# Four norms in two parts of the tokens, with 384-token ranges and weight splits taken ahead, in a two-block kernel on Trainium2

## The chip, the cores and the metric

The kernel runs on one core of one Trainium2 chip. The metric is device time in microseconds (us) of one execution. A core has TensorE (PE; its weight loads are shown apart as PEld), VectorE (DVE), ScalarE (ACT), GpSimd (POOL) and SyncE (SP), which here issues nearly all DMAs.

## The reference, cut to what matters

A first block (three mixers, output projection, MLP with squared relu) works on 512 tokens, then a second block of two layers on 512 tokens ("x") and 256 context tokens ("c"). Model width is 1024. Around the change this is computed (l is the layer of the second block):

```python
# first block
x = x + mix @ w_out
h2 = rmsnorm(x, norm2_w)                                  # "n2"
x = x + jnp.square(jax.nn.relu(h2 @ w_ff1)) @ w_ff2
# second block, l = 0 (x and context), then l = 1 (only x after the attention)
hx = modulate(rms_norm(x, norm1_g[l]), sh1, sc1)          # "n3" for l=0, "l1n1" for l=1
px = hx @ w_in[l]                                         # conv inputs, latents, fourier inputs
x = x + g1 * heads_out(att_x, px, hy, w_out[l])
x = x + g2 * sq_relu_mlp(modulate(rms_norm(x, norm2_g[l]), sh2, sc2), w_mlp1[l], w_mlp2[l])  # "l0n2", "l1n2"
```

rms_norm divides each token by the root of the mean of its squares over the 1024 features. In layer 1 the context is only needed up to keys and values, so "l1n1" norms 768 tokens and "l1n2" 512.

## The kernel before, in words

Activations lie feature-major: X is [128 partitions, 8 tiles of features, 768 tokens], the first 512 being x, the last 256 the context. Each weight matrix comes in tiles of 128x1024 fp32 through a ring of 5 (`weight_ring`), loaded by SP in the order of `loads` (`fill`, L2982). Each product is made of three fp32r products: ACT casts a tile to its high part (`split_hi`, L2182, row L2193) and DVE, or for every third tile POOL (`lo_of`), takes the low part (`split_lo`, L1352 and L2733, rows L1362 and L2743), into a ring of 4 (`WS`, "weight_split"). The activations have a high and a low part too. A slot of WS is free when the product four tiles earlier is done. `stage` on each engine splits up to two tiles ahead (AHEAD = 2).

TensorE's order is written out by hand, and each other engine has a program of its own that goes through the same steps; semaphores (`did`, `when`) tie them. `product` (L663, matmuls in L685) makes one 128-feature output tile over k = 0..7 and three parts; the token ranges are XB = (0..512, 512..768) where the context takes part and X1 = (0..512) elsewhere, so a range is one matmul with its own weight load. `product_as_made` (L635, matmuls in L654) makes two output tiles at once while the norm still makes the inputs: step k waits for the high part of feature tile k, and its low part is used a step later.

A norm stands between the output projection and the MLP (n2, l0n2, l1n2), or between the MLP and the next layer's in-projection (l1n1):

- DVE adds each output tile to X (`out_projection`, L1694; in the MLP L1738), ACT squares it (L2206), DVE sums the squares (L1373).
- TensorE's `norm` (L626) sums over partitions (`token_sums`, L603), filler matmuls (`keep_busy`, L589) keep it at work, ACT takes the root (L2211), DVE the reciprocal (L1378), TensorE spreads it to all partitions (L620).
- `normed_split` on DVE (L1380; L1388 scales, L1400 or L1402 takes the low part of even tiles), ACT (L2218; L2224 or L2226 makes the high part, L2230 the shifted whole of odd tiles) and POOL (L2748, L2753: the low part of odd tiles) makes the split inputs of the next product tile by tile, with two buffers in SQ.

All tokens go through a norm together, after the last output tile. `mlp` (TensorE L926) makes groups of 4 hidden tiles ("up", L685) and, one group later, adds them into X ("down", L949); the relu and the square of a hidden tile are made once for each range (ACT L2442 and L2446, POOL L2864, DVE L1721). Layer 0's down products run beside `late_modulation` on DVE (L1450).

SP's program stops at two norms: after w_ff1 tile 2 it waits until n2 has scaled its last tile (`n2_vec ("scaled", 7)`), loads two broadcast rows, and goes on with weights and modulation weights in turn; at l0n2 it waits for the last low parts.

In both attentions the first two tiles of w_out2 are split when head 7 begins (`feed`, L2094 and L2647: `split_hi`, `split_lo` up to `w_out2` 0 + 1). `mid` is the stage before the attention (spectra, values). The end of `attention_2` makes the first two output tiles as the mixes come (`out_pair`, L1292), and `MIX2` is the order of their k.

## Time and profile before

| | us |
|---|---|
| median of 3 timed runs | 2395.6 (2392.7 to 2411.45) |
| the profiled execution | 2409.31 |
| its span | 2407.5 |
| PE busy | 2305.8 (96% of the span) |
| DVE busy | 1409.9 (59%) |
| ACT busy | 901.5 (37%) |
| POOL busy | 514.6 (21%) |
| DMA | mean 95 GB/s, 227.69 MB |

Starts and windows are microseconds from the span's first instruction; durations in groups are ns of one instruction. A matmul's duration is from its issue to its modelled end, so back-to-back matmuls overlap and their pace is read from starts. In brackets stands how long the engine had been idle, and what ended that.

### The profile page before, as it was taken

How to read it: one execution, taken by the hardware profiler on the slowest of the kernel's cores; microseconds unless marked ns; L12 is line 12 of the kernel's file. 1: busy time of each engine (PE TensorE's matmuls, PEld its weight loads, DVE VectorE, ACT ScalarE, POOL GpSimd, SP SyncE). 2: the span in 40 equal slices, each digit the busy share in tenths (PEclk: the TensorE clock that was granted, in tenths of full speed). 3: DMA queues.
4: the chain of work that ended last, by engine and by line, in shares of the span. 5: the costliest groups of instructions: out<-in, count | busy, mean ns of one | idle time of the engine just before them, and what ended most of it. 6: DMA issues, size and time to landing. Idle time of an engine off the chain costs nothing.

```text
span 2407.5 us, 29863 instructions
## 1 busy us (share of the span) xinstructions
PE 2305.8 (96%) x11514; PEld 1828.8 (76%) x11514; DVE 1409.9 (59%) x2253; ACT 901.5 (37%) x1536; POOL 514.6 (21%) x385
## 2 busy tenths in 40 slices
PE   7989799999999998989999999999999999999998
PEld 5655577888877875668888888888776568888887
DVE  5475648888667456773565565543635774534435
ACT  4254533232333224882422222122422684423232
POOL 2332214232312210001312121111120001322221
PEclk9999899999999999999999999999999999999999
DMA  4211016555411221011243343321122112222321
GB/s 162 88 62 54 27 35 235 193 192 203 167 66 57 93 96 34 22 36 36 84 140 123 118 136 123 123 101 59 58 96 80 32 45 70 102 89 96 109 88 53
DMA packets 76248, 227.69 MB, mean 95 GB/s; under 512 B 9151, under 2 KB 12608, under 8 KB 76108
## 3 DMA queue, kind: packets, MB, share of 16 engines
q1 hardware_dynamic: 70928, 216.69, 26.5%
q0 software_dynamic: 1856, 6.07, 0.7%
q10 hardware_dynamic: 3324, 3.02, 0.4%
q8 instruction: 93, 1.52, 0.3%
q14 instruction: 47, 0.39, 0.1%
HBM read 220.99 MB, written 4.76 MB: 94 GB/s over the span
## 4 chain that ended last, share of the span: by engine, by line
PE 84%; DVE 7%; ACT 4%; issue 3%; POOL 2%; ACTq 0%; DMA 0%; DVEq 0%; SPq 0%; POOLq 0%
PE psum L685 33%; PE psum L949 25%; PE psum L1256 3%; PE psum L715 3%; PE psum L654 3%; PE psum L1287 2%; PE psum L735 2%; PE psum L1210 2%; PE psum L1145 1%; PE psum L1271 1%; PE psum L603 1%; PE psum L1104 1%; PE psum L1223 1%; PE psum L1171 1%; DVE mod_scratch L1440 1%
## 5 line engine op out<-in xcount | busy, mean ns | idle before, releaser
L685 PE MATMUL psum<-mix_split,weight_split 128*128 128x512 f32 (+1 forms) x3456 | 701.3, 364 | 2.3 <-POOL weight_split L2743 1.3
L685 PEld LDWEIGHTS psum<-mix_split,weight_split 128*128 128x128 f32 x3456 | 589.8, 188 | 110.4 <-POOL weight_split L2743 1.7
L949 PE MATMUL psum<-hidden,weight_split 128*128 128x512 f32 (+1 forms) x3072 | 623.2, 364 | 0.6 <-DVE residual L1736 0.6
L949 PEld LDWEIGHTS psum<-hidden,weight_split 128*128 128x128 f32 x3072 | 523.5, 188 | 96.9 <-DVE weight_split L1362 1.0
L2193 ACT CAST weight_split<-weight_ring 128x1024 fp32r<-128x1024 f32 x269 | 277.1, 1041 | 298.4 <-PE psum L949 235.6
L2743 POOL TENSOR_TENSOR weight_split<-weight_ring,weight_split 128x1024 fp32r<-128x1024 f32 x89 | 233.0, 2618 | 597.1 <-ACT weight_split L2193 596.5
L1721 DVE TENSOR_TENSOR hidden<-hidden_tmp,hidden 128x512 fp32r<-128x512 f32 (+1 forms) x128 | 156.0, 1238 | 305.9 <-POOL hidden_tmp L2864 305.9
L1362 DVE TENSOR_TENSOR weight_split<-weight_ring,weight_split 128x1024 fp32r<-128x1024 f32 x180 | 233.8, 1301 | 39.8 <-ACT weight_split L2193 39.8
L2864 POOL TENSOR_TENSOR hidden_tmp<-hidden_tmp 128x512 f32<-128x512 f32 (+1 forms) x128 | 127.5, 1007 | 598.3 <-ACT hidden L2446 598.0
L2442 ACT ACTIVATE hidden_tmp<-psum 128x512 f32<-128x512 f32 (+1 forms) x128 | 69.2, 541 | 482.8 <-PE psum L685 481.8
L1738 DVE SCALAR_TENSOR_TENSOR residual<-psum,modulation,residual 128x512 f32<-128x512 f32 x192 | 120.2, 657 | 156.3 <-PE psum L949 155.9
L685 PE MATMUL psum<-normed_in,weight_split 128*128 128x512 f32 (+1 forms) x936 | 186.7, 360 | 6.7 <-POOL weight_split L2743 3.6
L685 PEld LDWEIGHTS psum<-normed_in,weight_split 128*128 128x128 f32 x936 | 154.6, 194 | 41.9 <-DVE weight_split L1362 7.4
L1440 DVE CUSTOM_DVE_ANT_0 mod_scratch<-mod_ring,cond 128x1024 f32<-128x1024 f32 x96 | 130.7, 1362 | 1.7
L1256 PE MATMUL psum<-k_heads,q_heads 128*128 128x512 f32 (+1 forms) x288 | 107.4, 494 | 9.4 <-ACT mla_prob L2665 5.6
L2206 ACT ACTIVATE squares<-residual 128x512 f32<-128x512 f32 (+2 forms) x60 | 39.5, 659 | 180.7 <-DVE residual L1706 72.2
L715 PE MATMUL psum<-normed,weight_split 128*128 128x512 f32 x360 | 96.9, 421 | 6.0 <-ACT q_and_k L2344 4.5
L715 PEld LDWEIGHTS psum<-normed,weight_split 128*128 128x128 f32 x360 | 69.9, 201 | 32.9 <-issue 17.5
L1256 PEld LDWEIGHTS psum<-k_heads,q_heads 128*128 128x128 f32 x288 | 52.2, 195 | 52.7 <-issue 42.3
L2123 DVE TENSOR_TENSOR mla_probT<-psum,mla_probT 128x256 fp32r<-128x256 f32 (+1 forms) x144 | 72.0, 537 | 18.0 <-ACT mla_probT L2679 17.1
L2112 DVE TENSOR_REDUCE mla_stat<-psum 128x1 f32<-128x768 f32 (+1 forms) x80 | 67.7, 846 | 25.0 <-PE psum L1256 23.9
L2446 ACT ACTIVATE hidden<-hidden_tmp 128x512 fp32r<-128x512 f32 (+1 forms) x128 | 74.0, 578 | 8.4
(317 smaller groups left out, 2483.7 us busy)
## 6 DMA issues: line engine op xcount, KB each, us to landing
weight_ring<-in_w_mlp SPq DMA_DIRECT2D x128, 512.0 KB, 3.8
weight_ring<-in_w_ff SPq DMA_DIRECT2D x64, 512.0 KB, 4.4
mod_ring<-in_w_mod SPq DMA_DIRECT2D x48, 512.0 KB, 3.5
late_ring<-in_w_mod SPq DMA_DIRECT2D x96, 256.0 KB, 3.4
weight_ring<-in_w_in SPq DMA_DIRECT2D x45, 512.0 KB, 3.5
weight_ring<-in_w_out SPq DMA_DIRECT2D x24, 512.0 KB, 3.4
weight_ring<-in_tables SPq DMA_DIRECT2D x13, 512.0 KB, 3.5
weight_ring<-in_w_v SPq DMA_DIRECT2D x8, 512.0 KB, 3.9
```

Source lines behind the costliest of these rows:

```text
L685: m = pe.matmul(psum[:, b + r, 0:hi - lo], w[:, part_w, :], x[:, part_x, k, lo:hi], start=k == 0 and part_w + part_x == 0, stop=k == KT - ...
L715: m = pe.matmul(bank(b), w[:, part_w, :], HS_1[:, part_x, k, :], start=k == 0 and part_w + part_x == 0, stop=k == KT - 1 and part_w == 1)
L949: mm = pe.matmul(psum[:, b + r, 0:hi - lo], w[:, part_w, :], G[:, part_x, f % (2 * GROUP), lo:hi], start=jj == 0 and part_w + part_x == 0, ...
L1256: m = pe.matmul(psum[:, b + off // 512, 0:pw], QH[:, h % 3, q:q + P], KH[:, h % 3, k0 + off:k0 + off + pw], start=True, stop=True)
L1362: ve.tensor_tensor(WS[:, k, 1, 0:w], ring_of(i, 0, w), WS[:, k, 0, 0:w].bitcast(F32), ALU.subtract).then_inc(*did("split_lo_vec", j))
L1440: ve.tensor_tensor_reduce(out=mod_scratch[:, :], in0=mod_ring[:, n % 4, :], in1=cond[:, v, :], scale=1.0, scalar=0.0, op0=ALU.mult, op1=AL ...
L1721: ve.tensor_tensor(G[:, 1, k, a:z], act_tmp[:, f % 2, a:z], G[:, 0, k, a:z].bitcast(F32), ALU.subtract).then_inc(*did(tag + "_vec", ("lo", ...
L1738: ve.scalar_tensor_tensor(out=x, in0=ps, scalar=gate(m + i, a), in1=x, op0=ALU.mult, op1=ALU.add).then_inc(*did(tag + "_vec", ("down", g - ...
L2193: ac.copy(WS[:, j % SPLIT_RING, 0, 0:w], ring_of(i, 0, w)).then_inc(*did("split_hi", j))
L2446: ac.activation(G[:, 0, k, a:z], x, ACT.Square).then_inc(*did(tag + "_act", ("hi", f, r)))
L2743: po.tensor_tensor(WS[:, k, 1, 0:w], ring_of(i, 0, w), WS[:, k, 0, 0:w].bitcast(F32), ALU.subtract).then_inc(*did("split_lo_pool", j))
L2864: po.tensor_tensor(x, x, x, ALU.mult).then_inc(*did(tag + "_pool", ("square", f, r)))
```

## The change

It has five parts.

1. **Norms in two parts of the tokens.** n2 and l1n2 are cut into tokens 0..256 and 256..512, l0n2 and l1n1 into 0..512 and 512..768. The last four output tiles (of the last down group, all eight) are made first for part a, then for part b. Part a's sums come after tile (4, b) and its spread after (5, b) ((1, b) and (3, b) in the down group), and its `normed_part` runs beside the rest of part b's tiles. The first pair of the next product is made first over part a, then over part b, with part b's sums and spread between its steps. `keep_busy` is gone from these four norms.
2. **384-token ranges.** In layer 0's output projection (its first four tiles) and MLP (from hidden tile 2 on, down groups 0 to 6) the two ranges are 0..384 and 384..768. Relu, square and low part of a hidden tile are then one instruction over 768 tokens, and a residual add is three (`pieces_of`: 384, 128 and 256 wide).
3. **Splits ahead of the norm.** The first three weight tiles after a norm are split between the steps of its part a and part b (`last + 1` to `last + 3`).
4. **Splits ahead of the attention.** w_out2 tiles 0 and 1 are asked for at the start of `mid`, so that the stage-ahead rule splits them at the end of the in-projection, not in the attention.
5. SP waits for part b of n2 and of l0n2 where it waited for the whole norm.

```diff
-        LAST_APART = {"n1", "n2", "n3", "n3g", "l0n2", "l1n1", "l1n2", "fin"}
+        LAST_APART = {"n1", "n3", "n3g", "fin"}
+        PARTED = 4
+        def parts_of(norm):
+            cut = S if norm in ("l0n2", "l1n1") else S // 2
+            return [(norm + "a", 0, cut), (norm + "b", cut, T2 if cut == S else S)]
+        def up_spans(ranges, f):
+            return XB if len(ranges) > 1 and f < 2 else [(0, ranges[-1][1])]
+        def halves_of(l):
+            return X1 if l else [(0, T2 // 2), (T2 // 2, T2)]
...
+            def out_and_norm(tag, tiles, x, norm, order=range(KT)):
+                for i, p in product_in_parts(tag, tiles, x, [part[1:] for part in parts_of(norm)], order):
+                    if (i, p) == (4, 1):
+                        part_sums(norm, 0)
+                    if (i, p) == (5, 1):
+                        part_spread(norm, 0)
+            def pair_in_parts(tag, tiles, x, norm, evac, sums_at, spread_at):
...
+                for p, (part, lo, hi) in enumerate(parts_of(norm)):
...
+                    for step, _ in enumerate(steps):
+                        if (p, step) == (0, sums_at):
+                            part_sums(norm, 1)
+                        if (p, step) == (0, spread_at):
+                            part_spread(norm, 1)
...
+                                sums_at, spread_at = (1, 4) if len(ranges) > 1 else (2, 6)
...
 # TensorE, mid
+                for m in range(2):
+                    use_load("w_out2", (l, m), split=True)
...
 # VectorE, out_projection
+                add_part(4, 1)
+                inverse_part(norm, 0)
+                split_lo(last + 1)
+                add_part(5, 1)
+                split_lo(last + 2)
+                for t, _ in enumerate(normed_part(norm, 0, HS, gain, shift)):
+                    if t == 1:
+                        add_part(6, 1)
+                    if t == 3:
+                        add_part(7, 1)
+                inverse_part(norm, 1)
+                split_lo(last + 3)
+                for _ in normed_part(norm, 1, HS, gain, shift):
+                    pass
...
 # VectorE and ScalarE, attention
-                    if first and h == MH - 1:
-                        split_lo(load_at["w_out2", (l, 0)] + 1)
...
 # SyncE
-            sy.wait_ge(*when("n2_vec", ("scaled", KT - 1, 0)))
+            sy.wait_ge(*when("n2b_vec", ("scaled", KT - 1, 0)))
```

## Rows read from the trace of the kernel before

**Rows 1.** The page, part 4: shares of the chain that ended last, by engine.
```profile
PE 84%; DVE 7%; ACT 4%; issue 3%; POOL 2%; ACTq 0%; DMA 0%; DVEq 0%; SPq 0%; POOLq 0%
```

**Rows 2.** The chain in order of time, merged: start us, us, what.
```profile
1102.24 50.16 PE psum L685 x288
...
1228.99 33.92 PE psum L949 x192
...
2089.47 21.76 PE psum L949 x96
```

**Rows 3.** Timeline inside the second attention: start us, us, engine, line, tiles, shapes, count.
```profile
1926.06 1.20 PE L1287 MATMUL psum<-mla_probT,weight_split 128*128 128x256 f32 x8
...
1927.09 0.64 PE L1287 MATMUL psum<-mla_probT,v_heads 128*128 128x256 f32 x4
...
1927.56 1.03 PE L1223 MATMUL psum<-latents,weight_ring 128*128 128x256 f32 x4
```

**Rows 4.** Timeline at the norm l0n2 (brackets: idle before, releaser).
```profile
1152.34 1.48 PE L603 MATMUL psum<-squares,c_row 128*6 128x128 f32 x12
...
1156.42 0.94 DVE L1378 RECIPROCAL squares<-squares 6x128 f32<-6x128 f32 x1 [2.84 <-ACT squares L2211]
...
1160.88 17.24 PE L654 MATMUL psum<-mix_split,weight_split 128*128 128x512 f32 x96
...
1177.95 2.28 PE L685 MATMUL psum<-mix_split,weight_split 128*128 128x512 f32 x12
```

**Rows 5.** VectorE groups by form, 1100 to 1240 us: busy us, mean ns of one, idle before.
```profile
L1388 DVE SCALAR_TENSOR_TENSOR squares<-residual,gain_scale,psum 128x512 f32<-128x512 f32 x8 | 5.9, 744 | 1.3 <-PE psum L620 1.3
...
L1388 DVE SCALAR_TENSOR_TENSOR squares<-residual,gain_scale,psum 128x256 f32<-128x256 f32 x8 | 3.8, 476 | 0.0
```

**Rows 6.** Timeline at the norm n2.
```profile
345.40 1.04 PE L603 MATMUL psum<-squares,c_row 128*4 128x128 f32 x8
...
361.57 1.67 SPq L2994 DMA_DIRECT2D weight_ring<-in_w_ff  x3
...
365.11 7.14 PE L685 MATMUL psum<-mix_split,weight_split 128*128 128x512 f32 x30 [1.32 <-POOL weight_split L2743]
...
368.73 1.23 DVE L1362 TENSOR_TENSOR weight_split<-weight_ring,weight_split 128x1024 fp32r<-128x1024 f32 x1 [7.44 <-ACT weight_split L2193]
```

**Rows 7.** Timeline at the norm l1n2.
```profile
2038.44 1.04 PE L603 MATMUL psum<-squares,c_row 128*4 128x128 f32 x8
...
2056.67 3.56 PE L685 MATMUL psum<-mix_split,weight_split 128*128 128x512 f32 x15
```

**Rows 8.** Timeline at the norm l1n1 and the products after it.
```profile
1703.80 1.48 PE L603 MATMUL psum<-squares,c_row 128*6 128x128 f32 x12
...
1728.17 2.11 PE L685 MATMUL psum<-normed_in,weight_split 128*128 128x512 f32 x8 [2.54 <-POOL weight_split L2743]
...
1741.32 1.04 PE L993 MATMUL psum<-filter_h,s_fw 64*64 64x512 f32 x2 [0.74 <-ACT filter_h L2497]
```

**Rows 9.** Timeline inside the two attentions, at the early weight splits.
```profile
1064.68 2.80 PE L1256 MATMUL psum<-k_heads,q_heads 128*128 128x512 f32 x4 [2.59 <-ACT mla_prob L2665]
...
1965.09 1.20 PE L1287 MATMUL psum<-mla_probT,weight_split 128*128 128x256 f32 x8
...
1970.41 1.20 PE L1287 MATMUL psum<-mla_probT,weight_split 128*128 128x256 f32 x8
...
1971.33 2.00 ACT L2193 CAST weight_split<-weight_ring 128x1024 fp32r<-128x1024 f32 x2
...
1977.51 0.69 PE L1271 MATMUL psum<-c_ident,mla_prob 128*128 128x128 f32 x2 [3.70 <-DVE mla_probT L2123]
...
1981.92 1.67 PE L1287 MATMUL psum<-mla_probT,weight_split 128*128 128x256 f32 x8
```

**Rows 10.** Busy in a window: us, PE, PEld, DVE, ACT, POOL, clock, DMA, GB/s.
```profile
1805.00:1825.00 20.00, 20.00 (x97) 16.20 (x97) 7.10 (x9) 4.84 (x7) 0.34 (x1) 1.00 0.08 27
```

**Rows 11.** The page, part 5: the weight loads of L685.
```profile
L685 PEld LDWEIGHTS psum<-mix_split,weight_split 128*128 128x128 f32 x3456 | 589.8, 188 | 110.4 <-POOL weight_split L2743 1.7
```

More of the change, by code:

```diff
@@ L164 @@
 VEC, VECS = vec_plan()
+PART_OF = {f"{norm}{part}_{engine}": (f"{norm}_{engine}", part)
+           for norm in ("n2", "l0n2", "l1n1", "l1n2") for part in "ab" for engine in ("pe", "vec", "act", "pool")}
 class Ledger:
@@ L633, in norm, with product_as_made @@
                 freed[b] = freed[b + 1] = [last]
-            def product_as_made(tag, tiles, x, ranges, x_ready, evac, bs, at, order=range(KT)):
+            def product_as_made(tag, tiles, x, ranges, x_ready, evac, bs, at, order=range(KT), places=None, ends=True):
                 for k in range(KT + 1):
@@ L691, in product, with product_in_parts @@
                                 freed[b + r] = [evac(i, r)]
+            def product_in_parts(tag, tiles, x, spans, order=range(KT)):
+                at = [use_load(*w, split=True) for _, w in tiles]
+                for p, (lo, hi) in enumerate(spans):
+                    for (i, _), load in zip(tiles, at):
+                        j = split_at[load]
+                        b = bank_of[tag, i, p] = take()
+                        if p == 0:
+                            pe.wait_ge(*when(lo_of(j), j))
+                        wait_bank(b)
+                        for k in range(KT):
+                            w = WS[:, j % SPLIT_RING, :, order[k] * P:(order[k] + 1) * P]
+                            for part_w, part_x in ((0, 0), (0, 1), (1, 0)):
+                                m = pe.matmul(psum[:, b, 0:hi - lo], w[:, part_w, :], x[:, part_x, k, lo:hi],
+                                              start=k == 0 and part_w + part_x == 0, stop=k == KT - 1 and part_w == 1)
+                        m.then_inc(*did("gemm", (tag, i, p)))
+                        freed[b] = [(tag + "_vec", ("add", i, ("part", p)))]
+                        split_use[j] = (tag, i, p)
+                        yield i, p
@@ new lines, in out_and_norm @@
+            def out_and_norm(tag, tiles, x, norm, order=range(KT)):
[5 more added lines that the diff above has]
+            def pair_in_parts(tag, tiles, x, norm, evac, sums_at, spread_at):
+                bs = []
+                for i, _ in tiles:
+                    bs.append(take(2))
+                    bank_of[tag, i] = bs[-1]
+                at = [use_load(*w, split=True) for _, w in tiles]
+                for p, (part, lo, hi) in enumerate(parts_of(norm)):
+                    place = (0, 0) if p == 0 else (1, 0) if lo == S else (0, lo)
+                    steps = product_as_made(tag, tiles, x, [(lo, hi)], lambda k: part_ready(part, k), evac, bs, at, places=[place], ends=p == 1)
+                    for step, _ in enumerate(steps):
[3 more added lines that the diff above has]
+                            part_spread(norm, 1)
@@ L1322, in block_2 @@
                 RG = ranges_of(l)
-                if l == 1:
-                    norm("l1n1", 6, ("l1n1_vec", ("scaled", 7, 1)))
                 in_projection_2(l, "n3" if l == 0 else "l1n1")
@@ L1380, in normed_split, with normed_steps @@
             def normed_split(tag, HS, ranges, gain, shift, what="spread"):
+                for _ in normed_steps(tag, HS, ranges, gain, shift, what):
+                    pass
+            def normed_steps(tag, HS, ranges, gain, shift, what="spread"):
                 def scaled(t):
@@ L2423, in out_projection, with mlp @@
                     for m in ms:
-                        ac.wait_ge(*when(tag + "_vec", ("add", m, len(ranges) - 1)))
+                        ac.wait_ge(*when(tag + "_vec", ("add", m, last_piece(ranges, len(ranges) - 1))))
                         square(norm_tag, m, X[:, m, :], [SQ[:, 0, :], SQ[:, 1, :]], 0, ranges[-1][1])
-            def mlp(tag, w1, w2, G, act_tmp, ranges, work, sums, gained=None):
+            def mlp(tag, w1, w2, G, act_tmp, ranges, work, sums, gained=None, next_norm=None):
                 hi = ranges[-1][1]
@@ L2650, in feed @@
                     first = k0 == 0 and i == 0
-                    if first and h == MH - 1:
-                        split_hi(load_at["w_out2", (l, 0)] + 1)
                     if first and h % 2 == 0:
```

426 lines of the change are left out of this document (323 added, 103 removed).

## The prediction

> **What bounds the kernel now.** I read the page first: the chain that ended last lies on TensorE for 84% of the span [rows 1]. What can be won is TensorE's own pace, and the places where it waits or runs filler. The chain in order of time shows the pace [rows 2]. Where only 512 tokens are made, 96 matmuls take 21.76 us, 226.7 ns each. In layer 0's MLP, 96 pairs of a 512- and a 256-token matmul take 33.92 us, 353.3 ns a pair. The same kind of pair in layer 0's output projection is faster: 144 pairs in 50.16 us, 348.3 ns with the start and the end of the stretch in it, about 347 without. 256-token fp32r matmuls alone are seen in the attention: 8 of them from 1926.06 to 1927.09 (129 ns each), 4 from 1927.09 to 1927.56 (118 ns) [rows 3]. So N columns cost about N/2.4 ns + 13.3 (226.7 at 512, 120 at 256), and a 256-token matmul sometimes 7 to 9 ns more.
>
> Then the timeline at the four norms, from the first sums to the third product after the norm, where there should be only two products' work [rows 4, 6 to 8].
>
> **The 384-token ranges.** By that formula 384 columns are 173.3 ns and a pair 346.7, as the faster 512/256 pairs have; it saves 6.7 ns against 353.3. The pairs: up 30 tiles x 24 = 720, down 7 groups x 8 x 12 = 672; 1392 x 6.67 ns = 9.3 us. The output projection's four tiles already run at 346.7 and gain nothing. No row shows an fp32r matmul of 384 columns. From below, the excess of 6.7 ns may not come from the short range and stay: 0. From above I let it save twice as much, if the 13.3 is smaller too: 18. I take 9.3, since the 7 to 9 ns extra is seen on 256-column matmuls and not on 512-column ones.
>
> What a matmul costs apart from its columns can be set against a rule. The Trainium skill ("TensorE: Matmul & The Clock Gate", section Back-to-back issue gap) gives a warm matmul N/2.4 + 2.5 ns, a fixed cost that does not depend on how 768 columns are cut in two. By it the cut to 384 saves nothing; the rows agree neither on the 2.5 (they show 13.3) nor on its being fixed (353.3 beside 346.7 for the same columns). It is the first rival below.
>
> The other engines have room: a residual add becomes three instructions for two on DVE, some 0.2 us per tile of 4.2, and relu, square and low part become one for two; nothing of it is waited for. If that cover were gone, 56 tiles x 0.2 = 11 us would be the price.
>
> **The norms.** I set out each stretch in two clocks and let t = 0 be the end of tile (7, a), when all of part a's residual is made.
>
> *l0n2* [rows 4]. Before: four output tiles 4 x 24 x 0.3467 = 33.3; sums, fillers, root, reciprocal, spread 1152.34 to 1160.88 = 8.5; the pair to 1177.95 = 17.1; together 58.9. After: part a of four tiles 4 x 24 x 0.2267 = 21.8. From t = 0: (4, b) 2.9, sums 0.9, (5, b) 2.9, spread 0.5, (6, b) and (7, b) 5.8, so TensorE is at the pair at 13.0. Meanwhile ACT's root and DVE's reciprocal (0.94) end at 5.2, the add of (5, b) waits for the product (6.7), the split of the second weight tile (cast 1.04, low part 1.23) ends at 9.9, and part a's first tile is ready at 11.4: in time. But part b's sums stand at step 1 of the pair (TensorE at 15.3), and they need the add of (7, b), which on DVE stands behind two splits, the steps 0 to 3 of part a's norm (3 x 0.74 for two tiles [rows 5], 2.4 us with the hops between engines) and the add and sum of (6, b): it comes at 16.9, its square at 17.4. A stall of 2.1. Part b's root on ACT is queued behind all of part a's high parts (21.5), the reciprocal ends at 22.9, TensorE is at the spread at 22.0: a stall of 1.0. Part b runs at 3 x 0.48 us of DVE for two tiles [rows 5], no slower than TensorE's 0.72 a tile. The pair ends at 33.5. 58.9 - 21.8 - 33.5 = 3.6; 0.3 off for the slower 256-column matmuls: 3.3 gained.
>
> *n2* [rows 6]. Before: 21.8 + 19.7 (345.40 to 365.11) = 41.5. After: four tiles of part a at 2.88 = 11.5. The same walk gives the pair's start at 12.35, its part a until 20.2 (two stalls of 0.6), and part b bound by the norm: the chain scale, high part, low part on POOL takes, by an estimate from the 0.48 of DVE and half of what 512 tokens take on ACT and POOL, 1.7 us for two tiles, TensorE 1.44. The end is at 28.0. This is 39.5, but 256-column matmuls at 127 instead of 120 take back 1.0, and then comes SP: it waits for part b's last scaled tile and only then asks for w_ff1 tile 3. Before, that tile was asked for at 361.57 and its low part done at 369.96, 8.4 later, while TensorE needed it at 370.5, since it still had the waiting POOL split and tile 2 to do. Now TensorE ends the pair some 1.5 us behind the last scaled tile and tile 2 5.4 us after; it waits about 2.3 us. Together 42.8: 1 us lost.
>
> *l1n2* [rows 7]. Before 21.8 + 18.2 (2038.44 to 2056.67) = 40.0. After, no SP wait, and ACT's shifted parts pace part b: 11.5 + 27.5 = 39.0. 1 us gained.
>
> *l1n1* [rows 8]. Before: the last down group 33.9, then 1703.80 to 1728.17 = 24.4 (the pair's steps waited for ACT and the third weight tile for POOL's split, 2.54); 58.3. After: 21.8 for part a; from t = 0 sums at 2.9, (2, b) and (3, b) to 6.7, spread, the rest of part b to 13.0. DVE's norm of part a is broken by four adds with their sums, so step 2 waits 1.8 and the sums of part b 1.0; the pair ends at 28.2, and the third tile, split by POOL behind the root, is ready at 28.4. 58.3 - 50.2 = 8.1. Some of it goes back: part b's norm then still lies on DVE and ACT until about 33, ahead of the convolutions of the first two tiles and of the split of the fourth weight tile, needed at 35 and ready at 38.9. Behind it lies the filter chain, for which TensorE waits already (0.74 at 1741.32). I take off 3.9: 4.2 gained.
>
> The norms together: 3.3 - 1.0 + 1.0 + 4.2 = 7.5. Bounds: at worst the rate of the norm rules each pair and nothing is gained (0, and down to -5 with lower clock after each stall, as no filler stands there any more); at best every stall goes: the stretches less the pairs' own work are 8.8 (n2), 8.6 (l0n2), 7.3 (l1n2) and 13.5 (l1n1), 38.2, less 6 of sums and spreads and 4 of narrower matmuls, 28.
>
> **The early split of w_out2.** In layer 1's attention the groups of L1287 come 5.3 us apart (1965.09, 1970.41) and then 11.5 apart (1981.92), with two casts on ACT at 1971.33 (2.00) and TensorE idle 3.70 at 1977.51 [rows 9]. Without them the gap should be about the usual one; 5.5 of the 6.2 us is my value. Layer 0 has a smaller stall, 2.59 at 1064.68, of which I take 2.5. The splits go to the end of the in-projection, where TensorE is busy 20.00 of 20 us and ACT 4.84, DVE 7.10 [rows 10]: two casts (2.1) and two low parts (2.5) fit in, at no cost. Bounds 4 and 11; if ACT and DVE were full there, about 2 us a layer would be paid. 8.0 gained.
>
> **The sum.** 9.3 + 7.5 + 8.0 = 24.8, less 1 for short runs at the lower clock behind the new stalls: 23.8. From the profiled execution 2409.3 (span 2407.5 and 1.8 around it) it gives 2385.5. The median of the timed runs is 13.7 lower than that execution, so I predict 2395.6 - 23.8 = 2371.8, say 2372.
>
> **Rivals.**
> - *The 384-token ranges give nothing.* For it: a fixed cost per matmul; against it: the two paces above. 23.8 - 9.3 = 14.5, 2381.
> - *The norms hide nearly all.* If DVE's and ACT's queues are less in the way than I have them, little stalls but n2 on SP's load and the filters of layer 1 (7 of the 28): 21 instead of 7.5 from the norms, 2358. Against it: the place of the sums at step 1, behind four steps of DVE.
> - *A weight load is not hidden behind 256 columns.* A load lasts 188 ns [rows 11]. 816 of the 256-column matmuls now stand behind one another (output tiles 192 + 96 + 192, down 96, pairs 240). At 188 ns instead of 120 they cost 55 us more, and the kernel would be slower, 2427; from 150 ns a matmul on, the gain of 24 is gone. Against it: 4 to 8 of them at 118 to 129 in rows 3. A long run of them is not in the trace.
> - *The splits are simply late elsewhere* (the change of place does nothing), and l1n1 gives back all: 8 + 4 less, 2384.
>
> **How the numbers follow.** Forecast 0.45, 384 ranges nothing 0.18, norms hide nearly all 0.17, splits late elsewhere 0.15, weight load 0.05. The range goes from the second rival's 2358 to the case that the 384 ranges and two thirds of the rest (14.5) are missing, 2391. About 1% (24 us) is what a measurement of this kernel tells from no change, and 2372 lies at that edge: faster by over 1% is half the forecast's case (0.22), the hiding case (0.17) and a rest of the others (0.07); 0.46. Slower by over 1% 0.03, within 1% 0.51.
>
> **What would show it.** In the profile after: L685 and L949 pairs in layer 0's MLP at 346.7 ns (a group of 96 pairs in 33.28 us); no filler at the four norms but idle of 1 to 2 us ahead of part b's sums in l0n2 and l1n1; a wait for a weight_ring DMA of w_ff at the third or fourth product after n2; no ACT cast of a weight inside the attentions, and no gap over 1.5 us at head 7; TensorE waiting longer than 0.74 for the first filter sine of layer 1. Long runs of 256-column matmuls at over 150 ns, or groups still at 33.92, would prove the forecast wrong.

## The result, and the profile after

The kernel after takes 2386.1 us (median of 13 runs, 2381.9 to 2389.3); the kernel before, run 13 times (the three runs that the forecast knew among them), 2407.3 us (2392.7 to 2413.7). The ratio is 0.9913, with a 95% interval of 0.9898 to 0.9928 (so are all intervals in brackets behind a ratio below): 21 us less, where 23.8 were forecast, and a time inside the range (2357 to 2391). The median of 2395.6 us from which the forecast subtracted came from those three runs, two of them low; what sets runs of the kernel before some 10 of these 21 us apart is the main finding below (experiments 5 to 7); for the rest of their spread no cause was looked for.

The profiled executions differ by as much: spans of 2407.5 and 2385.4 us. Laid side by side stretch by stretch (a stretch goes from the start of one recognizable block of TensorE's chain to the start of another; all numbers us):

```
stretch                                     before    after   gained  forecast
n2: third out1 tile to third up group       108.91   110.52    -1.6    -1.0
attention, layer 0                          182.56   177.54    +5.0    +2.5 (early split)
l0n2: third out2 tile to third MLP tile      75.87    73.45    +2.4    +3.3
MLP of layer 0, to the last down group      491.84   482.56    +9.3    +9.3
l1n1: last down group to middle of layer 1  170.94   168.66    +2.3    +4.2
middle and attention, layer 1               164.98   160.72    +4.3    +5.5 (early split)
l1n2: third out2 tile to third MLP tile      50.96    51.28    -0.3    +1.0
```

The rows add to 21.4, the rest of the span changes by 0.7. The sum came nearly true; among the norms only l0n2 came near its term.

The page of the kernel after still has TensorE on the chain for 84%, as [rows 1]:

```profile
PE 2283.0 (96%) x11658; PEld 1889.0 (79%) x11658; DVE 1418.8 (59%) x2334; ACT 902.3 (38%) x1520; POOL 510.0 (21%) x363
...
PE 84%; DVE 7%; ACT 4%; issue 3%; POOL 1%; ACTq 0%; DMA 0%; DVEq 0%; SPq 0%; POOLq 0%
```

The chain in order of time, where [rows 2] had 33.92 us for 96 pairs, and a long run of 256-column matmuls (the case that the third rival needed, a weight load not hidden behind 256 columns):

```profile
1221.39 33.28 PE psum L1067 x192
1254.67 33.28 PE psum L755 x192
...
1994.55 14.39 PE psum L776 x120
```

96 pairs of 384 columns take 33.28 us, 346.7 ns each, as worked out; and 120 matmuls of 256 columns, each behind its own weight load, take 119.9 ns each, not 188. That rival is dead.

The timeline of TensorE at l0n2, which answers to [rows 4] (brackets: idle before, releaser):

```profile
1151.10 2.46 PE L724 MATMUL psum<-mix_split,weight_split 128*128 128x512 f32 x10
1153.49 0.60 PE L661 MATMUL psum<-squares,c_row 128*2 128x128 f32 x4
1154.75 0.60 PE L661 MATMUL psum<-squares,c_row 128*2 128x128 f32 x4 [0.67 <-ACT squares L2466]
...
1160.28 0.68 PE L678 MATMUL psum<-squares,c_ident 2*128 2x128 f32 x4 [0.61 <-DVE squares L1560]
1160.88 10.58 PE L724 MATMUL psum<-mix_split,weight_split 128*128 128x512 f32 x68
1171.30 5.02 PE L755 MATMUL psum<-mix_split,weight_split 128*128 128x384 f32 x28
```

The stalls stand where they were forecast, ahead of part b's sums and of its spread, but are smaller: 0.67 for 2.1 and 0.61 for 1.0.

The timeline at n2, which answers to [rows 6]:

```profile
363.53 1.67 SPq L3337 DMA_DIRECT2D weight_ring<-in_w_ff  x3
...
364.32 5.62 PE L755 MATMUL psum<-mix_split,weight_split 128*128 128x512 f32 x24
...
369.85 1.04 ACT L2440 CAST weight_split<-weight_ring 128x1024 fp32r<-128x1024 f32 x1 [6.75 <-DMA weight_ring<-in_w_ff]
370.93 1.23 DVE L1524 TENSOR_TENSOR weight_split<-weight_ring,weight_split 128x1024 fp32r<-128x1024 f32 x1 [7.93 <-ACT weight_split L2440]
...
372.21 29.12 PE L755 MATMUL psum<-mix_split,weight_split 128*128 128x512 f32 x120 [2.27 <-DVE weight_split L1524]
```

SP asks for w_ff1 tile 3, the fourth, at 363.53, 2 us later than before, while TensorE begins the third tile almost a microsecond sooner. It waits 2.27 us for the fourth; the forecast had 2.3. And the stall has a tail: 144 matmuls at 226.7 ns are 32.6 us, so from 364.32 with 2.27 of waiting the down products should begin at 399.2. They begin at 401.2.

At l1n1 TensorE (answers to [rows 8]) is at its third tile, L755 of 1706.56, 52.5 us behind the start of the last down group, where before it took 58.2. It then gives 3.4 of these 5.7 us back:

```profile
1706.56 5.74 PE L755 MATMUL psum<-normed_in,weight_split 128*128 128x512 f32 x24 [0.60 <-POOL weight_split L3065]
1714.84 1.94 PE L1130 MATMUL psum<-weight_ring,s_fw 33*64 33x512 f32 x2 [2.54 <-issue]
1718.10 7.42 PE L755 MATMUL psum<-normed_in,weight_split 128*128 128x512 f32 x24 [1.32 <-DVE weight_split L1524]
1725.44 1.07 PE L1138 MATMUL psum<-filter_h,s_fw 64*64 64x512 f32 x2
...
1754.83 1.02 PE L1161 MATMUL psum<-c_row,filter_h 128*128 128x1 f32 x8 [2.16 <-DVE filter_h L2082]
```

24 matmuls take 7.42 us at 1718.10 and 5.74 at 1706.56: the granted clock is lower. In these two stretches of the changed kernel, one at n2 and one at l1n1, the mean clock (third number from the right) is between the levels of 1.2 and 2.4 GHz (0.5 and 1.0), each time behind idle TensorE; in the 25 us behind the first of them it is 0.98:

```profile
372.20:376.00 3.80, 3.79 (x11) 3.03 (x12) 1.87 (x3) 3.74 (x6) 3.10 (x3) 0.65 1.03 417
```

```profile
1714.80:1725.50 10.70, 9.34 (x27) 5.97 (x28) 8.75 (x14) 3.50 (x4) 0.00 (x0) 0.68 0.30 98
```

### The profile page after: what moved, and what is told of

Its sections match the earlier page's. It is cut to its first block, busy times and chain, and to the rows that moved or that the text cites. A ratio compares the mean times of both kernels' runs of the same rounds, so it can differ in the third digit from the quotient of the medians.

```text
span 2385.4 us, 30256 instructions
## 1 busy us (share of the span) xinstructions
PE 2283.0 (96%) x11658; PEld 1889.0 (79%) x11658; DVE 1418.8 (59%) x2334; ACT 902.3 (38%) x1520; POOL 510.0 (21%) x363
## 4 chain that ended last, share of the span: by engine, by line
PE 84%; DVE 7%; ACT 4%; issue 3%; POOL 1%; ACTq 0%; DMA 0%; DVEq 0%; SPq 0%; POOLq 0%
PE psum L755 31%; PE psum L1067 24%; PE psum L829 3%; PE psum L1420 3%; PE psum L776 3%; PE psum L724 3%; PE psum L1451 2%; PE psum L849 2%; PE psum L1374 1%; PE psum L1309 1%; PE psum L1435 1%; PE psum L1091 1%; PE psum L661 1%; PE psum L1268 1%; PE psum L1387 1%
## 5 line engine op out<-in xcount | busy, mean ns | idle before, releaser
L755 PE MATMUL psum<-mix_split,weight_split 128*128 128x384 f32 (+1 forms) x3072 | 621.8, 363 | 3.6 <-DVE weight_split L1524 2.3
L755 PEld LDWEIGHTS psum<-mix_split,weight_split 128*128 128x128 f32 x3072 | 556.6, 188 | 65.1 <-DVE weight_split L1524 2.7
L1067 PE MATMUL psum<-hidden,weight_split 128*128 128x512 f32 (+1 forms) x2880 | 584.5, 363 | 0.0
L1940 DVE TENSOR_TENSOR hidden<-hidden_tmp,hidden 128x512 fp32r<-128x512 f32 (+1 forms) x98 | 141.8, 1449 | 319.5 <-POOL hidden_tmp L3201 319.5
L1524 DVE TENSOR_TENSOR weight_split<-weight_ring,weight_split 128x1024 fp32r<-128x1024 f32 x180 | 226.0, 1257 | 35.8 <-ACT weight_split L2440 35.8
L2737 ACT ACTIVATE hidden_tmp<-psum 128x512 f32<-128x512 f32 (+1 forms) x94 | 62.7, 667 | 479.6 <-PE psum L755 479.2
L1963 DVE SCALAR_TENSOR_TENSOR residual<-psum,modulation,residual 128x512 f32<-128x512 f32 (+3 forms) x232 | 117.8, 552 | 135.1 <-PE psum L1067 134.9
L755 PE MATMUL psum<-normed_in,weight_split 128*128 128x512 f32 (+1 forms) x936 | 185.8, 359 | 5.4 <-DVE weight_split L1524 3.9
L755 PEld LDWEIGHTS psum<-normed_in,weight_split 128*128 128x128 f32 x936 | 153.7, 193 | 41.5 <-DVE weight_split L1524 8.4
L829 PEld LDWEIGHTS psum<-normed,weight_split 128*128 128x128 f32 x360 | 69.5, 200 | 32.6 <-issue 17.5
L776 PE MATMUL psum<-mix_split,weight_split 128*128 128x256 f32 (+1 forms) x576 | 81.4, 302 | 0.0
L776 PEld LDWEIGHTS psum<-mix_split,weight_split 128*128 128x128 f32 x576 | 76.3, 191 | 5.0 <-issue 0.7
```

What stands on the lines that cost most here:

```text
L755: m = pe.matmul(psum[:, b + r, 0:hi - lo], w[:, part_w, :], x[:, part_x, k, lo:hi], start=k == 0 and part_w + part_x == 0, stop=k == KT - ...
L776: m = pe.matmul(psum[:, b, 0:hi - lo], w[:, part_w, :], x[:, part_x, k, lo:hi], start=k == 0 and part_w + part_x == 0, stop=k == KT - 1 an ...
L829: m = pe.matmul(bank(b), w[:, part_w, :], HS_1[:, part_x, k, :], start=k == 0 and part_w + part_x == 0, stop=k == KT - 1 and part_w == 1)
L1067: mm = pe.matmul(psum[:, b + r, 0:hi - lo], w[:, part_w, :], G[:, part_x, f % (2 * GROUP), lo:hi], start=jj == 0 and part_w + part_x == 0, ...
L1524: ve.tensor_tensor(WS[:, k, 1, 0:w], ring_of(i, 0, w), WS[:, k, 0, 0:w].bitcast(F32), ALU.subtract).then_inc(*did("split_lo_vec", j))
L1940: ve.tensor_tensor(G[:, 1, k, a:z], act_tmp[:, f % 2, a:z], G[:, 0, k, a:z].bitcast(F32), ALU.subtract).then_inc(*did(tag + "_vec", ("lo", ...
```

## The experiments

Theory after this reading: (1) the 384-token ranges give 9.3 us by TensorE's pace alone; (2) the early splits give 8 to 9; (3) the norms in parts give only about 3 net, because n2 waits for a load that SP asks for too late, and l1n1 gives back what it won to DVE and ACT. The rival to each: the ranges act through the shorter queues of ACT and DVE; the splits are late elsewhere; the norms are the main gain and the other parts give little. "Before" in the measurements is the kernel before, run beside the experiment on the same chip. Experiments 1 to 4 share one such series, 5 to 8 a second, 9 and 10 a third; 11 and 12 have one each. The changed kernel was run in none of them, so a difference from its median is one between two series. A gain is given by the ratio or by the medians, and the two differ by up to 3 us.

**1. The ranges alone.** The kernel before with this, and the residual adds cut at token 512:

```
-    product(f"out2_{l}", ..., HS_T2, RG, ...)
+    product(f"out2_{l}", ..., HS_T2, halves_of(l), ...)
...
-    mlp(f"mlp2_{l}", ..., HS_T2, G2, RG, tag)
+    mlp(f"mlp2_{l}", ..., HS_T2, G2, halves_of(l), tag)
```

> The kernel before with only the 384-token ranges (layer 0's output projection and MLP), unfused relu, norms and splits as before. Theory (a matmul of 512 beside one of 256 costs 353.3 ns a pair, two of 384 cost 346.7): 1392 pairs x 6.67 = 9.3 us less, ratio 0.9961; groups of 96 pairs at 33.28 us where before has 33.92. Rival, the third residual add and ACT's two relus bound the MLP: groups stay at about 33.9 and the gain is 0 to 2 us.

Measured: 2396.1 us (12 runs) against 2402.2 (27 runs), ratio 0.9982 (0.9968 to 0.9996). The profile says more than the times: the groups are at 33.28, and from the third MLP tile to the end of the last down group it takes 515.84 us where the kernel before took 525.76, 9.9 less (the third out2 tile to the third MLP tile is the same, 75.7 and 75.9). So the pace is right, and a third to a half of its worth is missing in the times (6.1 us less by the medians, 4.3 by the ratio). The two relus and three adds were left unfused; nothing waits for them.

**2. The early splits alone.** In the kernel before, the two loads behind `next_split[l]` in the middle, and the splits at head 7 of the attention taken out on DVE, ACT and POOL:

```
                 next_split[l] = len(split_use)
+                for m in range(2):
+                    use_load("w_out2", (l, m), split=True)
...
-                    if first and h == MH - 1:
-                        split_hi(load_at["w_out2", (l, 0)] + 1)
```

> The kernel before with only the early splits of the first two w_out2 tiles. Theory: the stall of TensorE at layer 1's head 7 (3.70 of a gap of 11.5 us between two groups of L1287 that otherwise stand 5.3 apart) goes and the one of layer 0 (2.59) too: 8.0 us by the forecast's terms (5.5 + 2.5), 9.3 by the two profiles (4.3 + 5.0), ratio 0.9961 to 0.9967. Rival, the splits are simply late elsewhere: 0, with a new stall of 2 us or more at the end of the in-projection or in the filters.

Measured: 2395.8 us (10 runs) against 2402.2, ratio 0.9963 (0.9940 to 0.9985): 8.9 us less by the ratio, 6.4 by the medians. Middle and attention of layer 1 take 159.75 us for 164.98 (5.2 less; forecast 5.5). Experiments 1, 5 and 6, which split as before, have 163.8 to 164.1 there, so against them it is 4.0 to 4.3. Layer 0's attention takes 180.71 for 182.56, 1.9 less; in experiment 3 it was 179.25, 3.3 less. No new stall appears in the in-projection. The forecast's term holds, and the rival "late elsewhere" falls.

**3. Both, with the norms whole.** The kernel before with the two diffs above.

> Both of the two edits before, the four norms whole as in the kernel before. If the parts add up and the norms are what is left of the whole change (21.3 us): by the two profiles the norms give 2.7 us (n2 -1.6, l0n2 +2.3, l1n1 +2.3, l1n2 -0.3), so this kernel gains 18.6, ratio 0.9923; by the forecast's own terms the norms give 7.5 and this kernel gains 14 to 17, ratio 0.993 to 0.994. If the norms hid nearly all (21 us), it would gain next to nothing.

Measured: 2389.4 us (6 runs) against 2402.2, ratio 0.9943 (0.9925 to 0.9961): 13.7 us less by the ratio, 12.8 by the medians. The changed kernel is 3.4 us lower by the medians and 7 by the ratios. That can't tell 2.7 us from 7.5, but the norms are the smaller part either way.

**4. The changed kernel with 512 and 256 again.**

```
-            return X1 if l else [(0, T2 // 2), (T2 // 2, T2)]
+            return X1 if l else XB
...
```

Relu, square and low part of a hidden tile stay one instruction over 768 tokens each.

> The changed kernel with the ranges put back to 512 and 256 tokens, all else as changed. Theory: 9.3 us slower than the changed kernel, so 12 us faster than before, ratio 0.995, and groups of 33.92 us again. Rival, the ranges matter only through the fused relu or the shorter queue of DVE: less than 4 us slower than the changed kernel.

Measured: 2395.2 us (12 runs) against 2402.2, ratio 0.9969 (0.9955 to 0.9984), 9.2 us above the changed kernel's median (13 by the two ratios). Groups at 33.92, so the pace doesn't come from the fused instructions. Against the other series the ranges are worth all of their 9.3 us; within this one they are worth less, 6.1 us in experiment 1 and 6.4 from experiment 2 to 3 (medians). The norms in parts, from experiment 2 to this one, are worth 0.6 us.

**5 and 6. The kernel before, twice more.** Why not all? Of the 27 runs of the kernel before in that series the six at a mean granted clock of 0.984 stand in two heaps: 2399.4 to 2400.5 us and 2408.0 to 2409.6. Both experiments are the kernel before, unchanged.

> The kernel before, word for word, for a second profiled execution. Its timed executions stand in two heaps at the same granted clock (at 0.984: 2399.4 to 2400.5 and 2408.0 to 2409.6 us), the kernel with 384-token ranges alone in one (2394 to 2402). Theory A: in some executions the 512/256 pairs run at 346.7 ns, in others at 353.3, so this profile shows layer 0's MLP groups of 96 pairs either all at 33.92 us with a time of 2402 or more, or at 33.28 with 2394 to 2401. Theory B: the two heaps come from somewhere else; the groups are at 33.92 in a fast execution too.

> The kernel before once more, a third profiled execution: as for the second one, groups of 33.92 us with a time over 2402, or of 33.28 us with one under 2401, if theory A holds; 33.92 in both if B does.

Measured: 2407.0 and 2400.3 us. The chain in order of time of experiment 5, from layer 0's norm on:

```profile
1159.59 17.15 PE psum L654 x96
1176.74 50.88 PE psum L685 x288
1227.62 33.92 PE psum L949 x192
```

and of experiment 6, the same kernel:

```profile
1161.47 16.88 PE psum L654 x96
1178.35 49.92 PE psum L685 x288
1228.27 33.28 PE psum L949 x192
```

The same program, the granted clock 1.00 in both, runs its 512/256 pairs at 353.3 ns in one execution and at 346.7 in the other, through the whole MLP: 525.8 us and 515.8. Theory A holds. Before this norm both ran at the faster pace (50.16 us for 144 pairs in the output projection), so the pace is chosen here and kept. Of the profiles with 512/256 pairs in this MLP, those of the kernel before and of experiments 2, 4, 5 and 10 have the slower pace throughout, that of 6 the faster one.

**7. What chooses it.** In the kernel before, one small matmul of 16 x g columns ahead of down group g of layer 0:

```
+    if tag == "mlp2_0" and m + i == 0:
+        pe.matmul(psum[0:32, b, 0:16 * g], C["ident"][:, 0:32], C["ident"][:, 0:16 * g], start=True, stop=True)
```

> The kernel before with one extra small matmul of 16 x g columns ahead of layer 0's down group g (g = 1 to 8), written to a bank that the next product clears. Theory A1, the pace of a 512/256 pair hangs on how the run of matmuls happens to start and lasts as long as nothing interrupts it: some of the groups behind an extra matmul take 33.28 us and others 33.92. Theory A2, it is fixed for the execution or for the shape: all groups stay at 33.92 (or all at 33.28) beside the extra 0.02 to 0.13 us each. Time within 1 us of before by A2, up to 9 us less by A1.

Measured: 2406.5 us (10 runs), ratio 1.0002 (0.9989 to 1.0015). The chain of its profile (L951 are the down groups, each with its extra matmul in front; L685 the up groups):

```profile
1177.25 49.92 PE psum L685 x288
1227.34 34.10 PE psum L951 x192
1261.44 33.92 PE psum L685 x192
1295.54 34.12 PE psum L951 x192
1329.66 33.92 PE psum L685 x192
1363.78 33.48 PE psum L951 x192
1397.26 33.28 PE psum L685 x192
```

It starts at the faster pace; the 16-column matmul puts it to the slower one, the 32-column one leaves it there, the 48-column one puts it back, and the later ones (64 to 128 columns) keep it at 33.28. Two flips within one execution, each at an extra matmul: A1. That fits a pace that hangs on how the run of matmuls happens to start; which starts give which pace was not tried, and what in the engine keeps it stays open. The times don't drop, so the extra matmuls are no cure. The 384-token ranges don't raise the best pace, which the kernel before has too in some executions; all seven profiles that have them show it.

**8. The load ahead of the wait, and later sums.** In the changed kernel:

```
-            fill(load_at["w_ff1", 2])
+            fill(load_at["w_ff1", 4])
             sy.wait_ge(*when("n2b_vec", ("scaled", KT - 1, 0)))
-                sums_at, spread_at = (1, 4) if len(ranges) > 1 else (2, 6)
+                sums_at, spread_at = (2, 5) if len(ranges) > 1 else (2, 6)
```

> The changed kernel with two edits at two norms: SP asks for w_ff1 tiles 3 and 4 ahead of its wait for n2b's last scaled tile, and in the pair after l0n2 part b's sums and spread stand behind steps 2 and 5 in place of 1 and 4. Theory: the 2.27 us idle ahead of the fourth product of n2 goes, since its weight comes 2 to 3 us earlier (from the start of the out1 tiles to the first group of 96: 110.5 to about 108.5 us); at l0n2 the stalls of 0.9 and 0.61 us go and the stretch takes 71.8 to 72.3 instead of 73.3. Together 3 to 3.5 us. Rival for the first: the cast on ACT stands behind the norm's high parts anyway, and the gain is under 1 us. Rival for the second: the idle time moves to the first steps of part b, 0.

Measured: 2377.6 us (6 runs) against 2406.2 (17 runs), ratio 0.9880 (0.9862 to 0.9898), 8.4 us below the changed kernel's median. TensorE at n2 and at l0n2:

```profile
355.40 8.13 PE L724 MATMUL psum<-mix_split,weight_split 128*128 128x256 f32 x56
363.36 31.92 PE L755 MATMUL psum<-mix_split,weight_split 128*128 128x512 f32 x140
```

```profile
1146.54 1.04 PE L661 MATMUL psum<-squares,c_row 128*2 128x128 f32 x8
1147.50 4.39 PE L724 MATMUL psum<-mix_split,weight_split 128*128 128x512 f32 x18
1151.97 0.68 PE L678 MATMUL psum<-squares,c_ident 2*128 2x128 f32 x4
```

No idle is left in either. l0n2 takes 72.1 us for 73.5, as expected. n2 takes 105.2 for 110.5: 5.4 us, where the stall that went was 2.27. Some 1.8 more is the tail at the lower clock (372.2 to 376.0 us at 0.65 and the next 25 us at 0.98 in the changed kernel, which is 1.3 and 0.5 us lost; at 1.00 here); the rest lies in the norm itself, where this execution was 1 us quicker. Experiment 4, with the load as late as in the changed kernel, takes 109.4 us there; against it the gain is 4.2. What the time dropped by beyond these 6.8 us lies in stretches that the edits don't touch (the first 24 products of layer 0's attention took 7.7 us for 9.0), and isn't claimed for them.

**9. l1n1's part b out of the filters' way.** In the kernel of 8, on DVE and ACT (POOL's share moved likewise):

```
-                for _ in normed_part(norm, 1, ...):
-                    pass
+                late_part.append(normed_part(norm, 1, ...))
+                late_steps(1, 2)
...
                 for i in range(2):
                     evac(i)
+                late_steps(l, 3)
...
                     next(filt, None)
+                    if i == 2:
+                        late_steps(l, 9)
```

> The kernel of e8 with the eight steps of l1n1's part b norm spread out on DVE, ACT and POOL: two ahead of the convolutions' evacuation of the first two in-projection tiles, three behind it, three behind the third tile's evacuation and the first filter step (before: all eight ahead of it). Theory: l1n1 in parts gives nothing (168.66 us from the last down group's start to the L1309 products of the middle, 168.85 with the norm whole) because part b's norm holds DVE and ACT from 1704 to 1712, ahead of the evacuation that frees the banks and of the filter chain; spread out, the first filter product starts 2 us earlier, the 2.54 and 1.32 us idle there go, and the stretch takes 164 to 167 us, 2 to 4 us off e8. Rival: the filter chain on DVE and ACT is the bound with or without it, or the pieces land in the filter chain's way: 168 to 170, no gain.

Measured: 2380.5 us (4 runs), ratio 0.9897 (0.9880 to 0.9915), and the stretch takes 171.3 us for 168.9 in experiment 8. TensorE's timeline:

```profile
1701.94 1.07 PE L1130 MATMUL psum<-weight_ring,s_fw 33*64 33x512 f32 x2
1705.41 7.15 PE L755 MATMUL psum<-normed_in,weight_split 128*128 128x512 f32 x24 [2.40 <-DVE weight_split L1524]
...
1716.51 11.22 PE L755 MATMUL psum<-normed_in,weight_split 128*128 128x512 f32 x48 [2.95 <-DVE weight_split L1524]
```

Half of my theory held: the first filter product no longer waits and comes 2.6 us earlier (58.2 us behind the last down group's start, 60.8 in the changed kernel). But the time isn't there: the next two products wait for their weight splits instead (2.40 and 2.95 us; 1.84 and 0.21 in experiment 8), which now stand behind the moved steps. Over the stretch TensorE's idle time falls only from 11.2 to 10.4 us, while its busy time for the same matmuls grows from 157.7 to 160.9, at a mean granted clock of 0.95 for 0.97. So the order won 0.8 us and not 2 to 4, and the 2.4 us that the stretch is longer are the clock's. The rival, no gain, holds; whether the moved waits brought the lower clock isn't shown.

**10. The early load in the kernel before.** The first line of 8's diff, `fill(load_at["w_ff1", 4])` for 2, in the kernel before.

> The kernel before (norm whole) with only SP's request for w_ff1 tiles 3 and 4 moved ahead of its wait for n2's last scaled tile. Theory: the load is late only because the parted norm made TensorE reach the fourth product sooner; here the stretch from the first of the out1 tiles to the first group of 96 stays within 1 us of 108.9 us. Rival: the early load is worth 2 us or more by itself, in the kernel before too (107 or less), and the 5.4 us that e8 won at n2 are not the parts' merit.

Measured: 2405.9 us (10 runs) against 2404.9, ratio 0.9993 (0.9973 to 1.0013). The stretch takes 107.0 us; other executions with the norm whole have 107.9 to 109.1. It is worth about 1 us there, and some 4 behind the norm in parts. The parts made the load late, and with it mended they gain 107.0 - 105.2, about 2 us, at n2, not -1.6.

**11. l1n1 whole, the rest as in 8.** The last down group, the norm and the in-projection's first pair as in the kernel before:

```
-                mlp(f"mlp2_{l}", ..., halves_of(l), tag, "l1n1" if l == 0 else None)
+                mlp(f"mlp2_{l}", ..., halves_of(l), tag)
...
+                if l == 1:
+                    norm("l1n1", 6, ("l1n1_vec", ("scaled", 7, 1)))
```

> The kernel of e8 with only l1n1 made whole again (last down group over all 768 tokens, fillers in the norm, in-projection pair behind it), the other three norms in parts. Theory: norming l1n1 in two parts gives nothing, because what TensorE saves up to the third in-projection tile (5 us) it waits again for splits and filters by the seventh: stretch from the last down group's start to the L1309 products 168.9 plus or minus 0.5 us and the time within 1 us of e8's 2377.6. Rival, the forecast's: the parts gain 4.2 us (or 2.3, as the first comparison had it), so this kernel is 2.3 to 4.2 us slower than e8.

Measured: 2378.0 us (6 runs), ratio 0.9876 (0.9847 to 0.9905): the same as 8 within what the intervals allow. The stretch, though, is 172.0 us in its profile. Its chain:

```profile
1705.96 7.37 PE psum L755 x24
...
1753.57 15.83 PE psum L755 x72
```

The same lines in experiment 3, whose l1n1 is whole too and whose stretch is 168.85 us:

```profile
1712.71 5.76 PE psum L698 x24
...
1758.83 14.14 PE psum L698 x72
```

The difference is the clock's: 24 matmuls in 7.37 us at 0.77, or in 5.76 at 1.00, and 1.7 us again in the x72. (Experiment 3 isn't free of dips: 24 matmuls take 8.62 us at 1749.42, and 7.03 in experiment 11.) Over all profiles, nine with l1n1 whole have 168.8 (twice) and 170.9 to 172.6 (seven times, up to 0.7 of it the slower pair); four with it in parts as in the change 168.7 to 168.9. So in this stretch its worth is 0 to 3 us, as the clock falls in the kernel with the norm whole. It costs elsewhere, which I had overlooked: behind it, middle and attention of layer 1 take 160.6 to 160.8 us in all five profiles with l1n1 in parts, and 158.9 in experiments 3 and 11 (159.75 in 2), where it is whole. The two stretches together are 329.4 to 329.7 us with the parts as in the change, 330.9 in experiment 11 and 327.8 in experiment 3. A gain that isn't in the times fits that. Neither of my two expectations is it alone.

**12. POOL's splits in halves.** In the kernel of 8:

```
+                    for c in (0, w // 2):
+                        m = po.tensor_tensor(WS[:, k, 1, c:c + w // 2], ring_of(i, c, c + w // 2), ..., ALU.subtract)
```

> The kernel of e8 with each of POOL's weight splits (1024 columns, 2.39 us) cut into two instructions of 512. What it tries: in the changed kernel DVE's low part of 256 columns, 0.48 us elsewhere, takes 2.48 us at l1n1 (start 1705.00) and 2.27 at l1n2 (2015.37), and each ends just as POOL's split ends (1706.51 beside 1707.48, and 2017.37 beside 2017.64). Theory: a DVE instruction with two SBUF inputs waits out the whole of POOL's instruction; with halves the two DVE instructions take at most about 1.5 us, and at l1n1 and l1n2 1 to 2 us are won, unless the two halves follow each other with no gap for DVE. Rival: with the halves back to back DVE is held for both, its instructions stay at 2.3 to 2.5 us and the time is within 1 us of e8's 2377.6, or 1 to 2 us above it for the 89 extra POOL instructions. The Trainium skill (SBUF - State Buffer, section SBUF: two separate sides) has the lock held for a whole instruction, which leaves open who takes it between two that follow at once.

Measured: 2377.1 us (4 runs), ratio 0.9867 (0.9843 to 0.9891), no different from 8. In the changed kernel, at l1n1, DVE's low part outlasts POOL's split and ends only behind POOL's next instruction:

```profile
1704.12 2.39 POOL L3065 TENSOR_TENSOR weight_split<-weight_ring,weight_split 128x1024 fp32r<-128x1024 f32 x1
...
1705.00 2.48 DVE L1589 SCALAR_TENSOR_TENSOR normed_in<-squares,modulation,normed_in 128x256 fp32r<-128x256 f32 x1 [0.19 <-ACT normed_in L2494]
...
1706.47 0.72 POOL L3075 TENSOR_TENSOR normed_in<-shifted,normed_in 128x256 fp32r<-128x256 f32 x1
```

With halves, DVE's low part and POOL's two halves at l1n1:

```profile
1695.31 2.62 DVE L1589 SCALAR_TENSOR_TENSOR normed_in<-squares,modulation,normed_in 128x256 fp32r<-128x256 f32 x1 [0.19 <-ACT normed_in L2494]
```

```profile
1694.42 2.53 POOL L3066 TENSOR_TENSOR weight_split<-weight_ring,weight_split 128x512 fp32r<-128x512 f32 x2
```

and at l1n2:

```profile
2005.95 1.17 DVE L1589 SCALAR_TENSOR_TENSOR mix_split<-squares,modulation,mix_split 128x256 fp32r<-128x256 f32 x1 [0.18 <-ACT mix_split L2494]
```

At l1n2 DVE got in between the halves (1.17 us for 2.27, and the stretch is 50.7 for 51.3); at l1n1 it ended at 1697.93, behind both (1696.95). The Trainium skill (SBUF — State Buffer, section SBUF: two separate sides) says that of a DVE instruction with two SBUF inputs and a GpSimd one that reads SBUF, whichever starts first keeps the other out for its whole length. The held instruction agrees with it: 0.48 us of work took 2.3 to 2.6 where POOL's split had started 0.4 to 0.9 us earlier. Which comes next, when POOL's instructions follow one another, differs: DVE's got in once here, and was passed over at l1n1 with halves and without. My expectation had each of the two ending with POOL's split; the one at l1n1 ended 1 us behind it.

## Why the prediction was right, and where its terms were not

- **The 384 ranges, 9.3 us: right in size for the profiled execution, wrong in kind.** "I take 9.3, since the 7 to 9 ns extra is seen on 256-column matmuls" took a state of that execution for a property of the shape. The row that said so was there: the same pairs at 348.3 ns in the output projection. The gain is 9.3 or 9.9 us in executions where the pair runs slowly and 0 where it does not, and 6 us between the medians of one series. That the profile to be subtracted from showed the slower pace is luck. The rule that I set against it (a fixed cost for each matmul) is half right: at the faster pace 512/256 and 384/384 cost the same 346.7 ns, so the cut itself saves nothing. Its fixed cost is not 2.5 but 13.3 ns here (226.7 at 512, 173.3 at 384, 120 at 256). The forecast also read the section too widely: the Trainium skill (TensorE: Matmul & The Clock Gate, section Back-to-back issue gap) gives that formula for a single matmul by itself, not for a stream of weight loads and matmuls as here.
- **The early splits, 8.0: right.** 4.0 to 5.2 us for 5.5 in layer 1, 1.9 to 3.3 for 2.5 in layer 0, 6.4 to 8.9 in the times; the 5.0 of the two profiles in layer 0 has the clock in it. They are hidden in the in-projection, as said.
- **l0n2, 3.3: about right** (2.4), by luck, since two errors stand against each other: the stalls were 1.3 us for 3.1, but part a's sums and spread, over 512 tokens, took 1.84 and 1.09 us where the walk had 0.9 and 0.5, and the pair began 1.8 us later.
- **n2, -1.0: right mechanism, short by 0.6** (the walk's own 42.8 less 41.5 is 1.3, entered as 1). The wait of 2.3 us for SP's load was in place and in size; missing was what a stall costs behind it, some 1.8 us at the lower clock. I had put 1 us for all of that in the sum.
- **l1n2, +1.0: wrong by 1.3.** The 256-column pace was 120 ns and better than feared, but POOL's weight split holds DVE's first step of part a's norm for 1.8 us, which no step of the walk had (experiment 12 gives back 0.6 of it).
- **l1n1, 8.1 less 3.9 given back: the 8.1 was mis-sized.** TensorE won 5.7 us by the third tile, not 8.1: the pair began 1.8 us late as in l0n2, and the tile 2.5 us behind the walk's 28.4. It lost all but 2.3 of it by the middle, 3.4 us for 3.9, to what was named, DVE's and ACT's queues ahead of evacuation and splits, and to the lower clock behind those waits (7.42 us for 5.75). Against experiment 3, at the same mean clock of 0.97, it won 5.2 and lost 5.0 (168.66 and 168.85). And middle and attention behind it take 1.7 to 1.8 us more than in experiments 3 and 11 in every profile with the parts, for which the forecast had no term.
- **The rivals.** Norms hide nearly all (2358): no, n2, l1n1 and l1n2 together gave 0.4. 384 gives nothing: true in some executions. Weight load not hidden: no, 119.9 ns. Splits late elsewhere: no. Two of the signs that I had named didn't show: ahead of part b's sums TensorE is idle for 0.67 us (l0n2) and 0.56 (l1n1), not 1 to 2, and it doesn't wait at the first filter sine of layer 1 (1725.44), but 2.54 us ahead of the filter product before it (1714.84).
- **The start, 2395.6.** Taking a difference of profiles off a median of three put the forecast 11.7 us low against the longer series (2407.3); another 2.5 come from the difference itself (23.8 for 21.3). Of the 14 us between 2372 and 2386.1 most is the base, and the range held it only because it was wide for other reasons: luck. Off the profiled execution the forecast was 2385.5, and the changed kernel's profiled execution took 2387.2.

Experiments 8, 11 and 12 are the fastest kernels here, 2377 to 2378 us: the change with the load asked for in time.

## What to carry to other kernels

When a wait is shortened, look at once which loads were asked for on the strength of the old timing: here one line on SP gave some 4 us, more than the 2.8 that all four norms in parts had. Price a stall of TensorE at up to double its length: the one of 2.27 us at n2 cost 1.8 more at the lower clock, while those of 0.6 and 0.7 in l0n2 cost nothing more (clock 1.00). And where executions of one kernel spread by more than others do, compare two profiles of the same kernel before explaining a difference between two kernels.

## What the runs showed of the hardware

- A 512-column fp32r matmul followed by one of 256 runs at 346.7 or at 353.3 ns a pair, at the same granted clock of 1.00; the choice holds for hundreds of microseconds, and in one execution it turned at an extra matmul of 16 and at one of 48 columns (experiments 5 to 7). Two of 384 columns were at 346.7 in all seven profiles that have them.
- The granted clock dips for some microseconds. Some dips differ between executions: the first product behind the pair at l1n1 took 5.7 us in the kernel before and in experiment 3, and 7.37 in experiment 11. One goes with the kernel: at the end of layer 1's attention the clock is 0.57 to 0.58 for 4 us in the changed kernel and in experiments 4, 8 and 12, and 1.00 in 2, 3, 9 and 11; the same 8 matmuls took 1.78 us at 1963.61 in the changed kernel and 1.22 us in experiment 11. TensorE idles 1.23 us just ahead of it and 1.22 in experiment 11, so its cause is open. The window in the changed kernel:

```profile
1963.60:1967.60 4.00, 3.99 (x20) 3.95 (x21) 2.23 (x6) 3.95 (x9) 1.28 (x1) 0.57 0.00 0
```

- A DVE instruction of 0.48 us with two SBUF inputs took 2.3 to 2.6 us beside POOL subtractions of 2.4 to 2.5.
